# Sliding-window attention in an encoder trunk: value products on 256 columns in two column strips, sinks as a score column, steps by key head with half of the query projection between them

## The reference, cut to what matters

```python
def sink_attention(q, k, v, valid, sinks):
    s = jnp.einsum('bqngd,bknd->bngqk', q, k).astype(jnp.float32)
    s = jnp.where(valid, s, -jnp.inf)
    sk = sinks.astype(jnp.float32).reshape(1, ATT_KV_HEADS, ATT_GROUP, 1, 1)
    m = jnp.maximum(jnp.max(s, -1, keepdims=True), sk)
    e = jnp.exp(s - m)
    p = e / (jnp.sum(e, -1, keepdims=True) + jnp.exp(sk - m))
    return jnp.einsum('bngqk,bknd->bqngd', p.astype(v.dtype), v)

def swa_prompt(h, k, v, w_q, sinks, w_o):      # queries scaled by 64 ** -0.5
    ...
    def one_chunk(c):                          # 8 chunks of 64 queries
        qs = lax.dynamic_slice_in_dim(q, c * CHUNK, CHUNK, axis=1)
        ks = lax.dynamic_slice_in_dim(kp, c * CHUNK, band, axis=1)   # band = 128 + 64 keys
        vs = lax.dynamic_slice_in_dim(vp, c * CHUNK, band, axis=1)
        valid = (c * CHUNK - WINDOW + jnp.arange(band)) >= 0
        return sink_attention(qs, ks, vs, valid, sinks)
```

## Time and profile before

| | kernel before |
|---|---|
| median of three runs | 1542.2 us |
| profiled execution | 1543.35 us |
| its span in the profile | 1541.6 us |
| TensorE matmuls busy | 1487.1 us (96%) |
| VectorE busy | 980.2 us (64%) |
| ScalarE busy | 566.4 us (37%) |
| GpSimd busy | 185.2 us (12%) |

### The profile page before, as it was taken

The page is one execution under the profiler, slowest core; times in us unless marked ns, Lnnn a source line. Parts: engine busy times, 40 slices in busy tenths (PEclk is TensorE's granted clock), DMA queues, the critical chain, the costliest instruction groups (busy, mean ns, idle before and its releaser), DMA issues.

```text
span 1541.6 us, 26228 instructions
## 1 busy us (share of the span) xinstructions
PE 1487.1 (96%) x10223; PEld 1445.8 (94%) x10223; DVE 980.2 (64%) x1754; ACT 566.4 (37%) x989; POOL 185.2 (12%) x196
## 2 busy tenths in 40 slices
PE   5999999999999999999998989999999999999997
PEld 5999889899999999999998967799999999999997
DVE  6345676548666666766677478626866666666656
ACT  4141475434323232333334157524433323232323
POOL 5002130120000000000023000021100000000000
PEclk9999999999999999999999989999999999999999
DMA  6422222532221221122204410021222222222102
GB/s 211 128 83 82 86 86 86 193 110 83 82 79 58 82 82 53 56 82 82 82 1 116 120 50 1 8 88 55 83 82 82 82 82 82 68 68 82 54 1 93
DMA packets 103638, 122.59 MB, mean 80 GB/s; under 512 B 12211, under 2 KB 96121, under 8 KB 103305
## 3 DMA queue, kind: packets, MB, share of 16 engines
q1 hardware_dynamic: 103576, 121.76, 24.4%
HBM read 109.89 MB, written 11.95 MB: 79 GB/s over the span
## 4 chain that ended last, share of the span: by engine, by line
PE 92%; DVE 6%; ACT 1%; issue 1%; DMA 0%; SPq 0%; DVEq 0%; ACTq 0%
PE ps L362 54%; PE ps L541 18%; PE ps L387 5%; PE ps L1791 3%; PE ps L1022 2%; DVE x_lo L451 2%; PE ps L1007 1%; PE ps L373 1%; PE ps L1300 1%; PE ps L987 1%; PE ps L1823 1%; DVE w_lo L349 1%; PE ps L1836 1%; DVE seq_states L2032 1%; DVE x_res L505 0%
## 5 line engine op out<-in xcount | busy, mean ns | idle before, releaser
L362 PE MATMUL ps<-x_hi,w_hi 128*128 128x320 f32 x1904 | 436.4, 310 | 12.4 <-DVE x_lo L451 6.9
L362 PE MATMUL ps<-x_lo,w_hi 128*128 128x320 f32 x1904 | 435.0, 310 | 0.0
L362 PE MATMUL ps<-x_hi,w_lo 128*128 128x320 f32 x1904 | 434.5, 309 | 0.0
L362 PEld LDWEIGHTS ps<-x_hi,w_hi 128*128 128x128 f32 x1904 | 318.9, 188 | 14.6 <-DVE w_lo L349 5.3
L362 PEld LDWEIGHTS ps<-x_lo,w_hi 128*128 128x128 f32 x1904 | 319.4, 188 | 0.0
L362 PEld LDWEIGHTS ps<-x_hi,w_lo 128*128 128x128 f32 x1904 | 319.3, 188 | 0.0
L342 ACT ACTIVATE w_hi<-w_raw 128x1024 fp32r<-128x1024 f32 x139 | 146.5, 1060 | 442.2 <-PE ps L362 393.1
L505 DVE TENSOR_TENSOR x_res<-x_res,ps 128x640 f32<-128x640 f32 x184 | 147.1, 817 | 121.0 <-PE ps L362 64.2
L349 DVE TENSOR_TENSOR w_lo<-w_raw,w_hi 128x1024 fp32r<-128x1024 f32 x139 | 172.4, 1245 | 29.6 <-ACT w_hi L342 22.2
L822 POOL TENSOR_TENSOR tail_cols<-up_rows,ones 128x4 f32 (+1 forms) x44 | 51.2, 1164 | 827.7 <-DVE up_rows L627 773.4
L625 DVE TENSOR_TENSOR up_rows<-ps,rstd_cols 128x320 f32<-128x320 f32 x88 | 43.1, 489 | 164.7 <-PE ps L362 164.7
(11 more groups left out here) (243 smaller groups left out, 1971.7 us busy)
## 6 DMA issues: line engine op xcount, KB each, us to landing
w_raw<-in_ffn_w_up_dram SPq DMA_DIRECT2D x44, 1024.0 KB, 5.2
d_raw<-in_ffn_w_down_dram SPq DMA_DIRECT2D x22, 1024.0 KB, 5.0
w_raw<-in_gla_w_in_dram SPq DMA_DIRECT2D x12, 1024.0 KB, 5.3
seq_states<-in_state_gla_dram SPq DMA_DIRECT2D x4, 1024.0 KB, 5.8
out_dram<-seq_states SPq DMA_DIRECT2D x4, 1024.0 KB, 6.7
w_raw<-in_gla_w_out_dram SPq DMA_DIRECT2D x4, 1024.0 KB, 7.4
w_raw<-in_att_w_q_dram SPq DMA_DIRECT2D x4, 1024.0 KB, 5.9
w_raw<-in_att_w_o_dram SPq DMA_DIRECT2D x4, 1024.0 KB, 5.2
```

Of the source, the lines that this page charges most:

```text
L362: mm = pe.matmul(PS[:, 2 * (u0 % 4) + f, 0:HALF], w[:, n0 % 4, k, :], x[:, k, f * HALF:(f + 1) * HALF], start=(k == 0 and a == 0), stop=(k ...
```

## The change

1. **Steps by key head.** The 32 prompt steps are ordered by key head g first, then by chunk c, then by half of the group (`step_of`: n = 16 g + 2 c + mp). Two neighbouring steps are a unit u with the same chunk and the same keys.
2. **Values of a unit.** One value product has 256 moving columns (the two steps of the unit side by side in `PT`), and its weights are the 64 value columns of the head. The score matrices a = 0 and a = 1 go to the two column strips of the array (`tile_position=(0, 64 a)`), and so to the lower and upper 64 partitions of the bank. Values run once in two iterations. `VZ` and `VS` have no zeros between, and GpSimd's part is gone.
3. **Sinks as a column.** The score tiles are 194 columns wide in PSUM; VectorE writes the sinks of a step's rows once into the column beside the scores, and the scores leave it there. The maximum is one instruction over keys and sink, negated; the exponentials' sum has the sink in it. L1164, L1166, L1167, L1172 and L1239 go. The scaling of the two matrices is one instruction.
4. **Sequences.** The scores are products of 64 rows by 64 columns in the two diagonal quarters of the array, the values eight products in two strips.
5. **Queries.** Only the tiles j = 0 to 3 (key head 0) are made ahead. The other four, 192 passes, stand in iterations 0 to 15: six after the scores and six after the transposes, in two banks of their own (`queries`). VectorE scales each half of 320 tokens for itself (`scale_queries`).
6. **Kept outputs.** While `XH` and `XL` still hold the input of the queries, the outputs of key head 0 are copied by VectorE into the place of their queries (`keep_out`); in iterations 21 to 29 they are rounded (`round_kept`, `rest_kept`).
7. **Output weights.** `round_tile` and `rest_tile` of the first four output weights stand in iterations 4, 8, 12 and 16, on VectorE between the maxima of n and the scaling of n-1.
8. **PSUM.** Until iteration 18 the transposes have one bank, and until unit 10 the outputs have one, where there were two of each.

```diff
-            for j in range(4, 8):
-                fm_tile(pe, T_AQ + j, u_q(j))
-            pe.wait_ge(s_vs, 16 * 2)
+            filled = [0]
+            def queries(upto):
+                while filled[0] < min(upto, 8 * R_MM):
+                    j, r = 4 + filled[0] // (2 * R_MM), filled[0] % (2 * R_MM)
+                    f, i = r // R_MM, r % R_MM
+                    if r == 0:
+                        pe.wait_ge(lo_done, T_AQ + j + 1)
...
+                    if i == 0 and f and j > 4:
+                        pe.wait_ge(free, u_q(j - 1) + 1)
+                    w, x = ((WH, XH), (WH, XL), (WL, XH))[i % 3]
+                    mm = pe.matmul(PS[:, query_bank + f, 0:HALF], w[:, (T_AQ + j) % 4, i // 3, :],
+                                   x[:, i // 3, f * HALF:(f + 1) * HALF], start=(i == 0), stop=(i == R_MM - 1))
...
             def scores(n):
...
+                        mm = pe.matmul(PS[:, score_bank(n) + a, o:o + nk],
+                                       QF[h, 2 * g + mp, c, :, :].rearrange("p m q -> p (m q)"),
                                        KTD[h, g, k0:k0 + nk], start=True, stop=True, tile_position=(HD * a, 0))
...
+                            mm = pe.matmul(PS[h, score_bank(n) + g, 0:WIN + SL],
+                                           QS[h, s, g, :, :].rearrange("p m t -> p (m t)"),
+                                           KCT[h, g, s, :], start=True, stop=True, tile_position=(HD * a, HD * a))
...
             def transposes(n):
...
-                if n >= 2:
-                    pe.wait_ge(a_pt, n - 1)
+                if n:
+                    pe.wait_ge(a_pt, n if n <= 18 else n - 1)
...
+            def values(u):
...
+                    for x, k in enumerate(parts):
+                        for a in range(2):
+                            mm = pe.matmul(PS[HD * a:HD * a + HD, b, 0:256], vv[0:k, t + x, g, :],
+                                           PT[0:k, u % 2, x, a, :], start=(x == 0), stop=(x == len(parts) - 1),
+                                           tile_position=(0, HD * a))
...
             for n in range(NATT + 3):
                 if n < NATT:
                     scores(n)
+                queries(12 * n + 6)
...
                 if 2 <= n < NATT + 2:
                     transposes(n - 2)
-                if n >= 3:
-                    values(n - 3)
+                queries(12 * n + 12)
+                if n >= 3 and (n - 3 >= NPR or n % 2 == 0):
+                    values(unit_of(n - 3))
...
+            def prompt_sinks(mp):
+                b = score_bank(mp)
+                v.wait_ge(free, (U_KC if mp else U_KT) + 1)
+                v.tensor_copy(PS[:, b:b + 2, 0:SW:SW - 1],
+                              SKP[:, :].rearrange("p (g m a) -> p a g m", g=2, m=2)[:, :, :, mp]).then_inc(sk_set, 1)
...
             def maxima(n):
                 v.wait_ge(a_sc, n + 1)
-                b = n % 2
...
+                v.tensor_reduce(NM[:, n % 2, :], score_view(n), AX.X, ALU.max, negate=True).then_inc(a_nm, 1)
...
             for n in range(NATT + 4):
...
+                if n < 16 and n % 4 == 2:
+                    v.wait_ge(q_half, n // 4 + 1)
+                    scale_queries(4 + n // 4, 0)
+                if 0 < n <= 16 and n % 4 == 0:
+                    rest_tile(v, T_AO + n // 4 - 1)
                 if 1 <= n <= NATT:
                     normalise(n - 1)
```

More of the change, by code:

```diff
@@ L1071, in step_of @@
         def step_of(n):
-            c, m = n // 4, 2 * (n % 4)
-            return c, m, m // 4
+            return n // 16, n % 16 // 2, n % 2
         def window(c):
@@ L1081, in key_parts, with key_cols, score_view, kept @@
                 return [WIN, SL]
-            nk = window(step_of(n)[0])[1]
+            nk = window(step_of(n)[1])[1]
             return [nk] if nk <= 128 else [128, nk - 128]
-        def heads_out(n, a):
-            b = out_bank(n)
-            if n < NATT - NS:
-                c, m, _ = step_of(n)
-                return [PS[:, b, 0:128].rearrange("p (m q) -> p m q", m=2)] + \
-                    [x[:, m:m + 2, CH * c:CH * c + CH] for x in (XH, XL)]
-            s = n - (NATT - NS)
-            h = slice(HD * a, HD * a + HD)
-            c = SEQ + SL * s
-            return [PS[h, b, 0:256].rearrange("p (g e m t) -> p g e m t", g=KVH, e=2, m=4)[:, :, a, :, :]] + \
-                [x[h, :, c:c + SL].rearrange("p (g m) t -> p g m t", g=KVH) for x in (XH, XL)]
-        def parts(n):
-            return range(1 if n < NATT - NS else 2)
+        def key_cols(n):
+            k = sum(key_parts(n))
+            if n >= NPR:
+                return slice(0, k)
+            o = 1 if n < NPR // 2 else SW - 1 - k
+            return slice(o, o + k)
+        def score_view(n, a=None):
+            b, k = score_bank(n), sum(key_parts(n))
+            o = 0 if n >= NPR or n < NPR // 2 else SW - 1 - k
+            if a is not None:
+                return PS[:, b + a, o:o + k + 1]
+            return PS[:, b:b + 2, o:o + k + 1]
+        def kept(k):
+            return QF[:, k // 2, 0:SEQ // CH, k % 2, :]
+        def heads_out(u):
+            b = out_bank(u)
+            if u < NPR // 2:
+                g, c, _ = step_of(2 * u)
+                return [PS[:, b, 0:256].rearrange("p (m q) -> p m q", m=4)] + \
+                    [x[:, 4 * g:4 * g + 4, CH * c:CH * c + CH] for x in (XH, XL)]
+            c = SEQ + SL * (u - NPR // 2)
+            return [PS[:, b, 0:128].rearrange("p (m t) -> p m t", t=SL)] + [x[:, :, c:c + SL] for x in (XH, XL)]
         def att_dve(v):
@@ new lines, in rest_kept, with rest_out @@
+            def rest_kept(k):
+                v.wait_ge(kept_hi, k + 1)
+                v.tensor_tensor(XL[:, k, 0:SEQ].rearrange("p (c q) -> p c q", q=CH), kept(k),
+                                f32(XH[:, k, 0:SEQ]).rearrange("p (c q) -> p c q", q=CH),
+                                ALU.subtract).then_inc(kept_lo, 1)
+            def rest_out(u):
+                if u < NPR // 4:
+                    keep_out(u)
+                    return
+                v.wait_ge(a_oh, u - NPR // 4 + 1)
+                i_, oh, ol = heads_out(u)
+                v.tensor_tensor(ol, i_, f32(oh), ALU.subtract).then_inc(a_ol, 1)
@@ L1203, in att_dve @@
                 if 1 <= n <= NATT:
                     normalise(n - 1)
-                if n >= 4:
-                    rest_out(n - 4)
+                if 22 <= n < 30 and n % 2 == 0:
+                    rest_kept((n - 22) // 2)
+                if n >= 4 and (n - 4 >= NPR or n % 2):
+                    rest_out(unit_of(n - 4))
             add_and_resplit(v, T_AO, U_AO, V_FFN + KT, XF[1])
-        def prob_cols(n, a):
-            return slice(256 * a, 256 * a + sum(key_parts(n)))
         def att_act(act):
@@ L1225, in att_act @@
                 round_tile(act, n)
-            for j in range(KT - 1):
+            for j in range(4):
                 act.wait_ge(full, u_q(j) + 1)
@@ L1266, in att_act, with round_kept, round_out @@
-            act.wait_ge(full, U_KC + 2)
+            def round_kept(k):
+                if k == 0:
+                    act.wait_ge(full, u_q(7) + 1)
+                    act.wait_ge(a_ol, NPR // 4)
+                act.activation(XH[:, k, 0:SEQ].rearrange("p (c q) -> p c q", q=CH), kept(k), ACT.Copy)\
+                    .then_inc(kept_hi, 1)
+            def round_out(u):
+                if u < NPR // 4:
+                    return
+                act.wait_ge(a_o, u + 1)
+                i_, oh, _ = heads_out(u)
+                act.activation(oh, i_, ACT.Copy).then_inc(a_oh, 1)
@@ L2134, in _ @@
                 add_squares(pool, k, 2)
-            att_pool(pool)
             clear_sums(pool, 3)
```

289 lines of the change are left out of this document (154 added, 135 removed).

## The result

The changed kernel takes 1525.2 us (median of four runs, 1522.0 to 1528.4) against 1542.1 of the kernel before (1541.3 to 1542.3): the ratio is 0.9889, with a 95% interval from 0.9869 to 0.991. It is 17 us faster, and the forecast was 10 us slower. The profiled execution took 1526.68, its span is 1524.8.

A forecast was written before the change was run, and what follows sets the result against it. The prediction took TensorE to bound the stage, with idling at its ends and its clock also costing. From the profiled 1543.35 us, plus 9.6 with the clock down, less 1.15 to the median, it forecast 1551.8 us, range 1522 to 1560.

The forecast's parts named there:

- The first 16 steps: Key head 0 with the query passes: S(16) starts at 922.1, some 9 us ahead, with three stalls of 1.1 us.
- The seam: At step 16: T(15) starts at 927.4 after TensorE idles 2.9 us, and the clock falls to 1.2 GHz.
- Strips overlap: Value products: two column strips run at once, a key part taking 0.58 us at full clock, 1.07 at half.
- The return of the clock: After the seam: 1.2 GHz holds until the output projection, making the kernel 9.6 us slower before the median correction; chance 0.53.
- Fall and return after 13.7 us: Rival for the clock after the seam: it falls but returns after 13.7 us, giving 1528 us; chance 0.17.
- the bound on the other side: After the seam: the clock returns after 13.7 us, as it did before the change.
- The output tile: First tile of the output projection: halves of 5.8 and 6.0 us at half clock, ending at 1016.6.
- The sink arithmetic: Four small VectorE operations a step and ScalarE work dropped: off the path at 1.2 GHz, worth 0.
- the full-clock sum: Steps from the seam on at 2.4 GHz: a pair takes 3.82 us, output tile ends at 988.1, total change -18.9 us.

The follow-up runs named there:

- gap in full-width steps: Idle VectorE reductions ahead of the scaling of step 25, against the changed kernel with its fourth output weight moved to iteration 34: 1523.6 us.
- strip by strip: Value passes of a unit run all in strip 0, then all in strip 1, against the kernel with all four output weights in iterations 33 to 36: 1538.4 us.
- sink work: Work like the former sink arithmetic put back, against the changed kernel with its fourth weight late and low parts behind the scaling in iterations 4, 8, 12: 1532.4 us.
- gap in the sequence steps: Idle VectorE reductions ahead of the scaling of step 32, against the changed kernel with its fourth output weight moved late, here to iteration 36: 1528.1 us.
- all weights late: All four output weights rounded in iterations 33 to 36, against the changed kernel's 4, 8, 12 and 16: 1526.6 us.
- queries ahead: The second half of the query projection put ahead of all steps again, against the kernel with all four output weights in iterations 33 to 36: 1531.1 us.
- passes of 128 columns: Each value pass of 256 columns made as two of 128, against the kernel with all four output weights in iterations 33 to 36: 1528.3 us.
- the repeat: Same kernel run again: changed kernel with the fourth weight in iteration 34 and low parts behind the scaling in iterations 4, 8, 12: 1514.5 us.

## Why the prediction was wrong

By its own steps:

- **The first 16 steps: right.** S(16) was forecast for 922.1 and started at 922.82, 53.25 us behind the first scores for 53.6; ahead of the kernel before by 9.1 for "some 9". The three stalls are 0.96, 0.73 and 0.72 for 1.1 each, their chain is the one named, and two moves showed it.
- **The seam: right.** T(15) at 928.00 for 927.4, idle 2.62 us for 2.9, and the clock falls behind it. The move of one weight takes both away.
- **Strips overlap: right.** 1.17 us for a value block where 2 x 0.58 was taken. Sequence steps 2.27 for 2.26 at full clock; a steady pair 3.67 for 3.82.
- **The return of the clock: wrong, and all else hung on it.** The step was "nothing like that stretch comes until the output projection. So I take 1.2 GHz from the seam to there". It took what ran before one return for what a return needs. The clock came back at 945.4 with values in half of the columns, six mode changes in two steps and full-width scores and transposes. The traces of this stage hold seven falls with prompt values still to come: each returned before these had ended, after 13.7 us before the change, 17.1 after it, 10.2, 20.5 and three times 3.4 in the experiments. Seven other falls came during the last prompt values or behind them, with only sequence work ahead, and all seven lasted to 3 to 5 us into the output tile (table behind this list). Sequence scores in between did not prevent a return as long as prompt values ran too: the clock came back at 964.0 with the gap in full-width steps, at 960.0 strip by strip and at 959.5 with the sink work, each time behind the first sequence scores. I had put both kinds of work under one rule.
- **The rival named what happened.** It is "Fall and return after 13.7 us", with 17.1 us and 1525.2 for 1528. So its number was near, but 3 us too high although the clock was down longer; the output tile and a pair (3.67 for 3.82) account for about that. It had 0.17, and the bound on the other side, a return as before, was in the text beside the choice. The only measured return of this stage spoke for it; a reason from the shape of the passes spoke against. The measured one should have had the larger share.
- **The output tile** got 3.4 us at 1.2 GHz where 6.8 were assumed from the earlier trace rows; a gain of 2.5 us that had no term. It is luck in part: behind the same wait of 0.70 us the clock fell in two of the twelve profiles that have it, and held in ten.
- **The sink arithmetic** was put at 0 for 1.2 GHz, which stays untested. At full clock, work of its size put back cost 7 us up to the sequence scores, 5 of them at least without the clock; the full-clock sum (3.82 a pair) had the chain without it and did not name its price.

The seven falls with only sequence work ahead (starts in the profile, us):

| run | falls at | output tile starts | back at |
|---|---|---|---|
| gap in the sequence steps | 956.5 | 979.2 | 983.8 |
| all weights late | 958.2 | 977.9 | 982.1 |
| queries ahead | 960.8 | 983.4 | 988.1 |
| passes of 128 columns | 956.0 | 978.5 | 983.3 |
| strip by strip | 970.2 | 989.2 | 994.1 |
| sink work | 969.7 | 983.8 | 986.8 |
| the repeat | 958.3 | 972.2 | 975.4 |

What stays open: what exactly a return needs. The runs tell steps with prompt values from sequence steps alone, but none changed one property of the work alone (columns, rows or mode changes) while the clock was down. Nor was it seen why the return took 3.4 us in one place and 20.5 in another, and two of the seven long stretches (17.1 us) are no longer than some that ended in prompt work; there only the place of the return speaks for the rule.

## What to carry to other kernels

A chain on other engines that stalled TensorE for 2 to 3 us cost three to five times its length here (8.3 us for 2.62, 7.5 for 1.70 and 0.55, 12.0 for 2.49 in the sequence steps), since the clock fell behind it: look for such chains where the cover of dense work ends, and move the casual work (here, a weight's rounding) out of them, one piece at a time and never several into a stage of small passes. Passes in different strips overlap only as neighbours, so alternate the strips. When TensorE's blocks shrink, the next chain is already waiting: small arithmetic that stood beside TensorE's long blocks without a gap of TensorE cost 5 to 7 us when it was put back beside the short ones.

## What the runs showed of the hardware

- TensorE's clock fell behind idle times of 2.62, 2.49, 2.01 and of 1.70 followed by 0.55 us, and held through 0.57 followed by 0.56. It also fell behind a series of 0.86, 0.53 and 0.97, and behind a single wait of 1.24 us that it survived in other kernels. In one program with waits of 1.24 and 0.67 us it fell in one execution and held in another, 7.1 us apart at the second output tile.
- Value passes of 256 columns in two 64-column strips: eight in 1.17 us in turn, 2.30 strip by strip; sixteen of 128 columns in 1.47.
- A fallen clock lasted 3.4 to 20.5 us where prompt blocks ran (full-width transposes, values in two strips), also with sequence scores between them. It lasted 14 to 23 us of sequence work alone (quarter-array scores, half-array values, TensorE busy for 27.20 of 27.30 us in one trace) and ended 3.0 to 4.9 us into the dense tile behind, in seven traces of seven.
